# Earlier top-k searches, four softmax batches and grid chunks on the load queue in a two-layer decoder with product-key experts

## What is computed

```python
def block(xb):                                   # 128 tokens
    q = (xb @ w_q).reshape(T, 8, 2, 128)
    s = einsum('thpc,hpnc->thpn', q, keys)       # 128 scores for each half, 8 heads
    sv, si = lax.top_k(s, 16)
    cand = (sv[:, :, 0, :, None] + sv[:, :, 1, None, :]).reshape(T, 8, 256)
    cv, ci = lax.top_k(cand, 16)                 # 16 experts per token and head
    eid = e1 * 128 + e2                          # of 16384 experts
    g = softmax(cv)
    a = einsum('td,thkd->thk', xb, u_tab[eid])
    coef = g * gelu(a)
    return einsum('thk,thkd->td', coef, v_tab[eid])
```

## Time and profile before

| | us |
|---|---|
| median of 3 runs | 3997.49 |
| lowest, highest | 3977.23, 3999.63 |
| the profiled execution | 4014.47 |
| its span, first to last instruction | 4012.7 |
| TensorE matmul busy | 3782.6 |
| VectorE busy | 2324.7 |
| ScalarE busy | 1744.0 |
| GpSimd busy | 1156.7 |

### The profile page before, as it was taken

One profiled execution on the slowest core, in us unless ns is written; L12 is line 12 of the kernel. 1 busy time (PEld: TensorE's weight loads), 2 busy tenths in 40 slices (PEclk: granted clock), 3 DMA queues, 4 the chain that ended last, 5 costly groups with the idle time before them and its releaser, 6 DMA issues.

```text
span 4012.7 us, 55614 instructions
## 1 busy us (share of the span) xinstructions
PE 3782.6 (94%) x18832; PEld 3180.7 (79%) x18832; DVE 2324.7 (58%) x3205; ACT 1744.0 (43%) x2116; POOL 1156.7 (29%) x727
## 2 busy tenths in 40 slices
PE   8999999999939999999999999999999849999998
PEld 8989887788837777777899889887878637787877
DVE  5564799854415555555565555899544425555555
ACT  5354444444414444444454544444444324444444
POOL 2100005888880000000111000018888840000000
PEclk9999999999979999999999999999999979999999
DMA  6666678898956666666565666778999846666665
GB/s 223 186 204 213 210 215 208 211 212 212 211 98 196 200 214 204 204 214 206 178 213 179 210 206 188 209 212 210 213 208 214 194 105 207 216 214 219 217 211 181
DMA packets 366400, 806.82 MB, mean 201 GB/s; under 512 B 113904, under 2 KB 177584, under 8 KB 365920
## 3 DMA queue, kind: packets, MB, share of 16 engines
q1 hardware_dynamic: 279376, 758.34, 61.9%
q0 software_dynamic: 86928, 47.23, 8.5%
HBM read 732.76 MB, written 40.11 MB: 193 GB/s over the span
## 4 chain that ended last, share of the span: by engine, by line
PE 55%; POOL 24%; DMA 9%; issue 6%; DVE 4%; ACT 2%; DVEq 0%; SPq 0%; ACTq 0%; POOLq 0%
POOL weight_grid L649 24%; PE ps L2141 9%; PE ps L2143 9%; PE ps L2142 9%; DMA w_raw<-in_v_tab 7%; PE ps L1775 4%; PE ps L1776 4%; PE ps L1777 4%; PE ps L2109 3%; PE ps L2111 2%; PE ps L2110 2%; DVE w_lo L1192 2%; DMA w_raw<-in_dense 1%; ACT w_hi L704 1%; PE ps L1858 1%
## 5 line engine op out<-in xcount | busy, mean ns | idle before, releaser
L1192 DVE TENSOR_TENSOR w_lo<-w_raw,w_hi 128x1024 fp32r<-128x1024 f32 x1312 | 1636.2, 1249 | 1467.8 <-ACT w_hi L704 1440.4
L704 ACT ACTIVATE w_hi<-w_raw 128x1024 fp32r<-128x1024 f32 x1312 | 1390.0, 1061 | 1957.0 <-DMA w_raw<-in_v_tab 833.3
L649 POOL DMA_INDIRECT weight_grid<-cv,idx x512 | 965.4, 1886 | 618.7 <-DVE cv L1639 457.5
L2109 PE MATMUL ps<-w_hi,act_lo_t 128*128 128x512 f32 x2048 | 805.7, 393 | 148.2 <-DVE w_lo L1192 135.9
L2141 PE MATMUL ps<-w_hi,act_lo_t 128*128 128x512 f32 x2048 | 806.9, 394 | 47.4 <-DVE act_lo_t L1686 46.4
L2143 PE MATMUL ps<-w_hi,act_hi_t 128*128 128x512 f32 x2048 | 800.7, 391 | 0.0
L2142 PE MATMUL ps<-w_lo,act_hi_t 128*128 128x512 f32 x2048 | 800.3, 391 | 0.0
L2110 PE MATMUL ps<-w_lo,act_hi_t 128*128 128x512 f32 x2048 | 798.7, 390 | 0.0
L2111 PE MATMUL ps<-w_hi,act_hi_t 128*128 128x512 f32 x2048 | 798.7, 390 | 0.0
L2109 PEld LDWEIGHTS ps<-w_hi,act_lo_t 128*128 128x128 f32 x2048 | 385.4, 188 | 249.9 <-DVE w_lo L1192 139.6
L2141 PEld LDWEIGHTS ps<-w_hi,act_lo_t 128*128 128x128 f32 x2048 | 386.2, 189 | 150.2 <-DVE w_lo L1192 62.1
(11 more groups left out here) (241 smaller groups left out, 2356.3 us busy)
## 6 DMA issues: line engine op xcount, KB each, us to landing
w_raw<-in_u SPq DMA_DIRECT2D x512, 512.0 KB
w_raw<-in_v_tab SPq DMA_DIRECT2D x512, 512.0 KB
w_raw<-in_dense SPq DMA_DIRECT2D x288, 512.0 KB
weight_grid<-gb SPq DMA_DIRECT2D x64, 512.0 KB, 5.4
gb<-weight_grid POOLq DMA_DIRECT2D x64, 512.0 KB, 6.2
big<-big SPq DMA_DIRECT2D x960, 32.0 KB
weight_grid<-cv,idx POOLq DMA_INDIRECT x512
x_spill<-big POOLq DMA_DIRECT2D x16, 256.0 KB, 4.9
```

Of the source, the lines that this page charges most:

```text
L649: pool.indirect_dma_start(grid, bass.IndirectOffsetOnAxis(ap=idx[:, n, k:k + 1], axis=0), cv[:, n, k:k + 1], None, compute_op=ALU.add).the ...
L704: act.activation(w_hi[:, slot, :], w_raw[:, slot, :], ACT.Copy).then_inc(s_hi, 1)
L1192: dve.tensor_tensor(w_lo[:, slot, :], w_raw[:, slot, :], w_hi[:, slot, :].bitcast(F32), ALU.subtract).then_inc(s_lo, 1)
L2109: pe.matmul(o, act_lo_t[:, kb, t], w_hi[:, s % 4, c], start=kb == 0, stop=False)
```

## The change

Constants: `EARLY = 3`, `BATCH_ENDS = (3, 7, 11, 16)`, `GB_PIECES = 8`, `EARLY_STEPS = (4, 4, 4, 3, 6, 2, 4)`.

- Three items are searched beside wq, over seven slabs each, from slab 10 on. Items 3 to 15 are searched beside turns 0 to 12 of u.
- Four softmax batches, ending at items 3, 7, 11 and 16. `less_max(0)` follows wq's last slab, `shares(0)` slab 7 of u. GpSimd waits for `s_slots` at the start of each batch.
- The u stage's loops on ScalarE and VectorE are written out.
- GpSimd loads only grid chunks 0 and 1. The others are loaded by SP, in eight DMAs of 64 KB (128 runs of 512 bytes), one behind each slab's load in v.

```diff
+EARLY = 3
+BATCH_ENDS = (EARLY, 7, 11, ITEMS)
+GB_PIECES = 8
...
+        def gb_piece(c, b, k):
+            n = P * T
+            q, half = k // 2, k % 2
+            o = c * (4 * n) + q * n
+            rows = grid[o:o + n] if isinstance(c, int) else grid[bass.ds(o, n)]
+            cols = slice(P * half, P * (half + 1))
+            return gb[:, b, T * q:T * (q + 1)][:, cols], rows.rearrange("(p t) a -> p (t a)", p=P)[:, cols]
...                                              # SP
+                def weights(c, b, k):
+                    if k == 0:
+                        sp.wait_ge(s_weighted, c + (U_TURNS * layer - 1))
+                    dst, src = gb_piece(c, b, k)
+                    sp.dma_start(dst, src).then_inc(s_gb[b], 16)
+                def v_chunk(c, b, ends=True, begins=True):
                     for s in range(8):
                         v_load(c, s)
-                        exchange(U_TURNS + c, c, s, c == 1, 2 * (1 - c))
+                        if s < 2 and ends:
+                            weights(c + 1, 1 - b, GB_PIECES - 2 + s)
+                        if s >= 2 and begins:
+                            weights(c + 2, b, s - 2)
+                        if isinstance(c, int) and c < 2:
+                            exchange(U_TURNS + c, c, s, c == 1, 2 * (1 - c))
...                                              # GpSimd
-                    if n % PER_BATCH == 0:
-                        pool.wait_ge(s_slots, BATCHES * layer + n // PER_BATCH + 1)
+                    if n == 0 or n in BATCH_ENDS:
+                        pool.wait_ge(s_slots, BATCHES * layer + (BATCH_ENDS.index(n) + 1 if n else 0) + 1)
...
-                def weights(c):
-                    if c >= 2:
-                        pool.wait_ge(s_weighted, U_TURNS * layer + c - 1)
-                    pool.dma_start(gb[:, c % 2, :]..., grid_chunk(c)...).then_inc(s_gb[c % 2], 16)
+                for c in range(2):
+                    for k in range(GB_PIECES):
+                        dst, src = gb_piece(c, c, k)
+                        pool.dma_start(dst, src).then_inc(s_gb_first[c], 16)
...
+                for c in range(BACK):
+                    back(c)
...                                              # ScalarE
+                def exponents(k):
+                    act.wait_ge(s_cvs, BATCHES * layer + k + 1)
+                    act.activation(cv[:, batch(k), :], cv[:, batch(k), :], ACT.Exp).then_inc(s_cexp, 1)
                 def u_turn(i, first=0):
                     for s in range(first, 8):
...
+                        if i == 0 and s == 6:
+                            exponents(0)
+                        if s == 3 and i + EARLY - 1 in BATCH_ENDS[1:]:
+                            exponents(BATCH_ENDS.index(i + EARLY - 1))
                 u_turn(0, first=4)
-                u_turn(1)
-                with act.Fori(0, 2) as j:
-                    for c in range(2, 5):
-                        u_turn((j, c))
...
+                for i in range(1, U_TURNS):
                     u_turn(i)
...                                              # VectorE
-                dve.wait_ge(s_sc, 16 * layer + 3)
-                for tb in range(TB):
-                    topk_turn((0, tb), qbase + 16 + 8 * tb, range(8))
+                for n, first in enumerate((10, 17, 24)):
+                    dve.wait_ge(s_sc, 16 * layer + 2 * (n // TB) + 3)
+                    topk_turn(n, qbase, range(first, first + 7), EARLY_STEPS)
+                lo(3, qbase + 31)
+                less_max(0)
                 ahead(ubase)
                 dve.wait_ge(s_sc, 16 * (layer + 1) + 1)
                 for s in range(RING):
                     lo(s, ubase + RING + s)
+                shares(0)
...
+                for i in range(SHUFFLED):
+                    n = i + EARLY
+                    beside = {}
+                    if i and n in BATCH_ENDS:
+                        beside[7] = lambda n=n: shares(BATCH_ENDS.index(n))
+                    if i == SHUFFLED - 1:
+                        beside[4] = lambda: weigh(0, 0)
+                    if n < ITEMS:
+                        topk_turn(n, ubase + 8 * (i + 1), range(8), TOPK_STEPS, i, beside)
+                    else:
+                        quads_turn(i, beside)
+                    if n + 1 in BATCH_ENDS:
+                        less_max(BATCH_ENDS.index(n + 1))
```

More of the change, by code:

```diff
@@ L86 @@
 TOPK_STEPS = (4, 4, 2, 3, 3, 6, 1, 4)
+EARLY_STEPS = (4, 4, 4, 3, 6, 2, 4)
 SLAB = 1024
@@ L262, in decoder_kernel @@
         s_gb = [S(f"s_gb{b}") for b in range(2)]
+        s_gb_first = [S(f"s_gb_first{b}") for b in range(2)]
         s_weighted = S("s_weighted")
@@ L361, in grid_chunk, with batch @@
             return rows
+        def gb_piece(c, b, k):
[5 more added lines that the diff above has]
+            return gb[:, b, T * q:T * (q + 1)][:, cols], rows.rearrange("(p t) a -> p (t a)", p=P)[:, cols]
+        def batch(k):
+            return slice(BATCH_ENDS[k - 1] if k else 0, BATCH_ENDS[k])
         def quads_of(j, b):
@@ L480, in v_load @@
                     load(s % RING, c * 8 + (n0 + s), rows.rearrange("a p n -> (a p) n"))
-                for c in range(2):
+                def weights(c, b, k):
[4 more added lines that the diff above has]
+                def v_chunk(c, b, ends=True, begins=True):
                     for s in range(8):
                         v_load(c, s)
-                        exchange(U_TURNS + c, c, s, c == 1, 2 * (1 - c))
-                with sp.Fori(2, U_TURNS - 1) as c:
-                    for s in range(8):
-                        v_load(c, s)
+                        if s < 2 and ends:
[4 more added lines that the diff above has]
+                            exchange(U_TURNS + c, c, s, c == 1, 2 * (1 - c))
+                v_chunk(0, 0, False)
+                v_chunk(1, 1)
+                with sp.Fori(1, U_TURNS // 2 - 1) as j:
+                    for b in range(2):
+                        v_chunk(j * 2 + b, b)
+                v_chunk(U_TURNS - 2, 0, True, False)
                 for s in range(8):
@@ L1090, in gelu @@
                         act.activation(stage[:, :], bank(u_bank(i, tb)), ACT.Gelu).then_inc(s_gelu, 1)
+                def exponents(k):
+                    act.wait_ge(s_cvs, BATCHES * layer + k + 1)
+                    act.activation(cv[:, batch(k), :], cv[:, batch(k), :], ACT.Exp).then_inc(s_cexp, 1)
                 def u_turn(i, first=0):
                     for s in range(first, 8):
-                        hi(s % 4, lin(i, 8, ubase + s))
+                        hi(s % 4, ubase + 8 * i + s)
                         if s == 1:
[L1096 to L1104, removed]
+                            gelu(i - 1, 0, True)
+                        if s == 4 and i:
+                            gelu(i - 1, 1, True)
+                        if i == 0 and s == 6:
+                            exponents(0)
+                        if s == 3 and i + EARLY - 1 in BATCH_ENDS[1:]:
+                            exponents(BATCH_ENDS.index(i + EARLY - 1))
                 act.wait_ge(s_spill, 16 * PIECES * (layer + 1))
                 u_turn(0, first=4)
-                u_turn(1)
-                with act.Fori(0, 2) as j:
-                    for c in range(2, 5):
-                        u_turn((j, c))
[L1112 to L1116, removed]
-                    u_turn(i)
[L1118 to L1122, removed]
+                for i in range(1, U_TURNS):
+                    u_turn(i)
                 vbase = SLAB0["vt", layer]
@@ L1590, in weigh @@
                         dve.wait_ge(s_shuffled[b], c * 128 + (256 * (SHUFFLES[b] * layer + 1) - 128 * b))
-                    dve.wait_ge(s_gb[b], c * 8 + (16 * (U_TURNS // 2 * layer + 1) - 8 * b))
+                    if isinstance(c, int) and c < 2:
+                        dve.wait_ge(s_gb_first[c], 16 * GB_PIECES * (layer + 1))
+                    else:
+                        dve.wait_ge(s_gb[b], c * (8 * GB_PIECES) + (16 * (U_TURNS // 2 - 1) * layer - 8 * b) * GB_PIECES)
                     rows = big[:, c * CHUNK:(c + 1) * CHUNK] if isinstance(c, int) else big[:, bass.ds(c * CHUNK, CHUNK)]
@@ L1607, in turn_quads, with topk_turn @@
                     dve.transpose(quads_of(i, b)[:, tb, :], stage[:, :]).then_inc(s_mix, 1)
-                def topk_turn(item, n0, slabs, turn=None, b=None):
+                def topk_turn(item, n0, slabs, counts, turn=None, beside=None):
                     steps = topk_steps(item)
@@ L1613, in topk_turn @@
                     tk_count[0] = 0
-                    for s in slabs:
+                    for s, some in zip(slabs, counts):
                         lo(s % 4, n0 + s)
                         if turn is not None and s in (2, 6):
-                            turn_quads(turn, s // 6, b)
-                        for _ in range(TOPK_STEPS[s]):
+                            turn_quads(turn, s // 6, turn % 2)
+                        for _ in range(some):
```

(24 more changed lines are left out.)

22 lines of the change are left out of this document (7 added, 15 removed).

## The result

The changed kernel takes 3800.8 us, median of four runs (3792.6 to 3803.4), against 3990.9 for the kernel before with one more run of it counted (3977.2 to 3999.6): a ratio of 0.952, 95% interval 0.949 to 0.956. The forecast was 3796. The profiled execution took 3792.6 us.

A forecast was written before the change was run, and what follows sets the result against it. TensorE, busy 94%, was taken to lose time to late scatters ending u, chunk bursts in v and Gelu table loads. 131.9 + 3 - 4 + 13 + 58 = 202 us, from the median 3997.5 to 3796, range 3770 to 3830.

The forecast's parts named there:

- The holes: End of each layer's u stage: TensorE's waits of 68.1 and 63.8 us go with scatters begun earlier, 131.9 us.
- the slow clock behind them: After each layer's u-stage wait, TensorE runs partly at 1.2 GHz; this goes too, 3 us for both layers.
- the spare time: End of u: last scatter ends at 1043, needed at 1139.7, so 93 us to spare, about as many in layer 1.
- Rival (b): u stage: scatters stretch beside searches and eat the slack, needing 2.61 us each; 3931 us, chance 0.05.
- The third search: q projection: some 9 us of VectorE's time, hidden in its idle time; without that cover 9 us a layer.
- the further batches: u stage: two more less_max and shares a layer, some 1.4 us of VectorE each; hidden, or 3 us a layer.
- the waits in ScalarE's queue: ScalarE waits in exponents ahead of hi and a Gelu; VectorE is nearly done and the ring holds three slabs: nothing.
- The 4 us for scatters beside searches: u stage: scatters lie beside searches for longer, slowing TensorE's matmuls; about 2 us a layer, bounds 0 and 8.
- The v stages: v: grid chunks in eight 64 KB pieces behind the loads remove 58 of 62.1 us of weight-load waits.
- Ring slack: v: a chunk delays a load by up to 2.35 us, TensorE stops 1.19, so the ring has some 1.2 us.
- Written-out loops: ScalarE's u loop: Gelu table loads in each pass go, 8 x 1.6 = 13 us; bounds 0 and 16.
- The sum: Whole kernel: 131.9 + 3 - 4 + 13 + 58 = 202 us gained, forecast 3796 us; chance 0.72.

The follow-up runs named there:

- start5: Changed kernel with batches ending at 5, 8, 12 and 16, shares(0) behind slab 31 of u: 3805.5 us, 0.951.
- start7: Changed kernel with three batches ending at 7, 11 and 16, shares(0) behind slab 47 of u: 3850.1 us, 0.961.
- alone: Kernel before with only the grid chunks in eight pieces on the load queue, batches, searches and loops as before: 3944.2 us, 0.991.
- undone: Changed kernel with grid chunks loaded as before, one 512 KB DMA each on GpSimd's queue: 3839.3 us, 0.965.
- e_exp_earlier: Kernel before with exponents(1) on ScalarE moved between turns 14 and 15 of u: 4017.3 us, 1.005.
- the halves: Changed kernel with two DMAs of 256 KB a grid chunk, behind slabs 2 and 6: 3835.2 us, 0.962.
- e_actloop: Changed kernel with ScalarE's turns 16 to 30 of u as a hardware loop of five passes of three turns: 3796.0 us, 0.953.
- whole chunks: Changed kernel with each grid chunk loaded by one 512 KB DMA on the load queue, behind slab 2: 3829.8 us, 0.960.

## Why the prediction was right

- **The holes.** 131.9 us forecast and 3 for the slow clock behind them; the two together measured 131.6, and by the mechanism given: the first scatter began at 460.75 (463 forecast), the last ended at 1054.7 (1043). The scatters took 1.99 us instead of 1.95, with their issue 2.3 instead of 2.25, so GpSimd hardly rested and the spare time was some 68 us, not 93. The start5 and start7 runs show that the spare time is real and where it ends. Rival (b) asked for 2.61 us a scatter.
- **The third search, the further batches, the waits in ScalarE's queue.** Costed at nothing, and nothing is seen: u's slab 0 comes at 438.2 instead of 440.4, the first 250 slabs of u take less time than before. The 4 us for scatters beside searches can't be told apart in that.
- **The v stages.** 58 us forecast. In the profiled executions 66.3 us went; in medians, the part was worth 35 us (alone) and 49 us (undone). The mechanism is right, shown by both. The size is the term that was off, by 9 to 23 us in medians. It came from the waits of one execution, slower than all the timed runs, and was taken off their median. Against that execution it was short by 8 us, the clock that the longest stops cost, which the forecast had for the holes and not for v. That a usual run had fewer such stops was not shown: e_exp_earlier, on another chip, has 55.7 us of them in an execution of 3992.7 us.
- **Ring slack.** Read as 1.2 us from one stop, and wrong: the halves put it well under 1.2. The forecast didn't hang on it, since a piece delays a load by 0.3 us.
- **Written-out loops.** 13 us forecast; the u stages got 18.9 us shorter, and the waits for `stage` fell from 23.7 us over the whole span to 0.7, and to 5.5 and 5.9 in the changed kernel's two further profiles. But the step "the u loop's table loads go because the loop is written out" named the wrong cause. The loads came from a loop entered with `Exp`'s table; a turn between `Exp` and the loop removes them too. Where the holes stand, e_exp_earlier gained nothing; that the loads cost time once the holes are gone follows from the waits and was not run by itself. What of the 18.9 us is the tables and what VectorE's plain code was not separated; e_actloop puts ScalarE's looping itself at 6 us, within the noise.
- **The sum.** 202 us forecast, 190 by the medians, 222 by the profiled executions. In the profiled executions the terms beside the v stages gave 156 us where 144 were forecast, and v gave 66 where 58 were. In medians the whole is 12 us under the forecast, which v alone covers. That 3796 came within 5 us of 3800.8 is in part luck: the start was taken as 3997.5, and one more run put it at 3990.9, so an error of 7 us in the start and one of 12 in the gain cancel in part.

Two rules of the Trainium skill bear on this. "DMA: Bandwidth & Descriptors", section Bandwidth, says to batch transfers to 1 MiB or more; it points the wrong way here. Eighths beat whole chunks by 36 us, as the small transfers are hidden and the stops behind a large one are not. "SBUF — State Buffer", section "SBUF: two separate sides", says that GpSimd can't write descriptors while VectorE's fp32 copies hold the port that the two share. That would show as slower scatters beside searches; with 165 us more of such company they rose from 1.95 to 1.99 us, little.

## What to carry to other kernels

A wait that ends a stage is to be followed to the start of the slow chain behind it, not to its end: here to when the first batch of weights is ready. If that chain has an own rate, the hole is its end less the other's arrival, and speeding up the other engine only widens the hole until the chain begins earlier. Beside a ring of loads with little slack, cut other transfers down to what the slack takes and spread them, whichever queue they go on; find the size by trying two or three, not from one stop.

## What was not expected

- 256 KB twice a chunk cost as much as 512 KB once (41 and 36 us), 128 KB four times nothing that the medians can tell.
- The runs of a kernel lie closer together with chunks in pieces: 10 us over six runs and 11 over four, against 34 over eleven for the kernel before in the same group, and 18 over four for chunks on GpSimd's queue. The bursts' cost varies from run to run, so one profiled execution is a poor measure of it. Part of that is the clock: of the four runs with chunks on GpSimd's queue, which has no holes, the two fastest had a mean clock of 0.998 and the two slowest, 9 to 18 us longer, 0.995 and 0.996, which is 8 to 12 us of clock.
- Moving one `Exp` by a turn in the kernel before made it 0.5% slower while the trace of its fastest run shows fewer waits. Not explained.
